# A gated state-space and convolution layer on one core: the last projection's two token parts become 336 and 240 columns wide, where they were 288 each

## The reference

```python
proj = x @ w_in                       # 2048 -> 10240, split into eight parts
y_a  = ssm_branch(u_a, ...)           # complex state space, GELU, GLU
y_a  = (y_a * silu(z_a)) @ w_out_a    # 1024 -> 2048
y_c  = conv_branch(b_c, c_c, h_c, ...)
y_c  = (y_c * silu(z_c)) @ w_out_c    # 1024 -> 2048
merged = sigmoid(g_a) * y_a + sigmoid(g_c) * y_c
out  = merged @ w_o                   # 2048 -> 2048, the last projection
r    = DN_ALPHA * x + out             # residual
mu   = mean(r); var = mean((r - mu)**2)        # over the 2048 features
y    = (r - mu) * rsqrt(var + 1e-5) * ln_g + ln_b
```

## Time and profile before

| | |
|---|---|
| median of three runs | 1619.18 us (1614.2 to 1620.25) |
| profiled execution | 1611.43 us, of which 1609.6 us are the span |
| TensorE busy | 1576.2 us, 98% of the span |
| VectorE busy | 820.9 us, 51% |
| ScalarE busy | 443.2 us, 28% |
| chain that ended last | TensorE 93%, VectorE 5% |
| first pass of the last projection | about 1378.0 to 1481.2 us |
| second pass | about 1481.2 to 1584.8 us |
| after the last matmul of a half | 1584.8 to 1609.6 us |

### The profile page before, as it was taken

One profiled execution on the slowest core, in us unless ns is written; L12 is line 12 of the kernel. 1 busy time (PEld: TensorE's weight loads), 2 busy tenths in 40 slices (PEclk: granted clock), 3 DMA queues, 4 the chain that ended last, 5 costly groups with the idle time before them and its releaser, 6 DMA issues.

```text
span 1609.6 us, 27311 instructions
## 1 busy us (share of the span) xinstructions
PE 1576.2 (98%) x11878; PEld 1571.0 (98%) x11878; DVE 820.9 (51%) x1148; ACT 443.2 (28%) x566; POOL 189.0 (12%) x348
## 2 busy tenths in 40 slices
PE   8999999999999999999999999999999999999994
PEld 8999999999999999999999999999999999999993
DVE  5976374464463563543533523123742355566887
ACT  4222222222222222222222222222421122333444
POOL 0110041131211311212212212010000000000000
PEclk9999999999999999999999999999999999999997
DMA  9352262352443543534634535244544433456572
GB/s 306 100 162 92 88 173 74 110 150 70 134 117 101 137 122 111 166 99 125 174 97 140 150 84 160 81 145 157 182 143 131 132 123 116 157 184 194 184 224 101
DMA packets 87448, 221.23 MB, mean 137 GB/s; under 512 B 19744, under 2 KB 28576, under 8 KB 87328
## 3 DMA queue, kind: packets, MB, share of 16 engines
q1 hardware_dynamic: 71456, 188.78, 37.1%
q0 software_dynamic: 15872, 30.70, 8.1%
HBM read 186.55 MB, written 28.16 MB: 133 GB/s over the span
## 4 chain that ended last, share of the span: by engine, by line
PE 93%; DVE 5%; SPq 1%; DMA 1%; issue 1%; ACT 0%; DVEq 0%
PE acc L618 88%; DVE w_lo L947 1%; SPq L404 1%; DMA w_raw<-in_w 1%; PE y_ps L662 0%; PE y_ps L663 0%; PE y_ps L661 0%; DVE r_all L1437 0%; PE y_ps L660 0%; PE y_ps L659 0%; PE v_ps L638 0%; PE v_ps L639 0%; PE v_ps L637 0%; PE y_ps L658 0%; DVE r_all L1436 0%
## 5 line engine op out<-in xcount | busy, mean ns | idle before, releaser
L618 PE MATMUL acc<-xh,w_hi 128*128 128x288 f32 x2560 | 556.0, 298 | 5.6 <-DVE xl L955 3.3
L618 PE MATMUL acc<-xl,w_hi 128*128 128x288 f32 x2560 | 553.4, 297 | 0.0
L618 PE MATMUL acc<-xh,w_lo 128*128 128x288 f32 x2560 | 552.5, 297 | 0.0
L947 DVE TENSOR_TENSOR w_lo<-w_raw,w_hi 128x1024 fp32r<-128x1024 f32 x263 | 321.6, 1224 | 408.1 <-ACT w_hi L736 406.5
L736 ACT ACTIVATE w_hi<-w_raw 128x1024 fp32r<-128x1024 f32 x263 | 277.8, 1058 | 607.3 <-PE acc L618 592.5
L618 PEld LDWEIGHTS acc<-xh,w_hi 128*128 128x128 f32 x2560 | 414.7, 190 | 8.1 <-issue 4.3
L618 PEld LDWEIGHTS acc<-xh,w_lo 128*128 128x128 f32 x2560 | 415.3, 190 | 0.0
L618 PEld LDWEIGHTS acc<-xl,w_hi 128*128 128x128 f32 x2560 | 415.2, 190 | 0.0
L618 PE MATMUL acc<-mh,w_hi 128*128 128x288 f32 x512 | 151.4, 296 | 0.0
L618 PE MATMUL acc<-mh,w_lo 128*128 128x288 f32 x512 | 150.7, 294 | 0.0
L618 PE MATMUL acc<-ml,w_hi 128*128 128x288 f32 x512 | 150.7, 294 | 0.0
(11 more groups left out here) (272 smaller groups left out, 1543.8 us busy)
## 6 DMA issues: line engine op xcount, KB each, us to landing
w_raw<-in_w SPq DMA_DIRECT2D x263, 512.0 KB, 3.8
sg_dram<-out_st SPq DMA_DIRECT2D x32, 288.0 KB, 4.5
v_sw<-v_st POOLq DMA_DIRECT2D x32, 144.0 KB, 4.9
gc_in<-sg_dram SPq DMA_DIRECT2D x16, 288.0 KB, 2.7
sz_in<-sg_dram SPq DMA_DIRECT2D x16, 288.0 KB, 2.8
x_in<-in_xT SPq DMA_DIRECT2D x32, 144.0 KB, 2.2
outT<-o_st SPq DMA_DIRECT2D x32, 144.0 KB, 1.8
mb<-mq_dram POOLq DMA_DIRECT2D x8, 512.0 KB, 6.9
```

The source lines that it names most:

```text
L618: ins = pe.matmul(acc[:, par, t, 0:TH], w, m[:, k0 + k, t * TH:(t + 1) * TH], start=first and k == 0 and n == 0, stop=last and k == KH - 1 ...
L947: dve.tensor_tensor(w_lo[h % NW][:, :], w_raw[:, h % NW, :], w_hi[h % NW][:, :].bitcast(F32), ALU.subtract).then_inc(lo_ready, 1)
```

## The change

The two token parts get the widths `TO = (336, 240)`. The part widths enter the matmuls of the last projection, the feature sums, and every VectorE and ScalarE operation on `r_all`, `pivot`, `sq`, `acc_d`, `acc_q`, `mean`, `rstd`, `mean_r` and `o_st`. The input slots `x_in` become four tiles of 336 columns, where they were two tiles of 576 used by halves. Each engine issues the same instructions in the same order as before; only their widths and the tiles' places differ. The halves of all earlier projections keep their two matmuls of 288 columns.

```diff
+TO = (336, 240)
-    x_in = [r(f"x_in{i}", [P, TOK]) for i in range(2)]
+    x_in = [r(f"x_in{i}", [P, TO[0]]) for i in range(4)]
-    o_st = r("o_st", [P, 8, TH])
+    o_st = r("o_st", [P, 8, TO[0]])
-    def of_half(x, t):
-        return x[:, t * TH:(t + 1) * TH]
+    def of_part_o(x, t):
+        return x[:, t * TO[0]:t * TO[0] + TO[t]]
     def x_slot(m):
-        return of_half(x_in[m % 4 // 2], m % 2)
+        return x_in[m % 4][:, 0:TO[m // KX]]
...
-        def half(h, par, mh_, ml_, k0, first, last, per_block=None, ts=(0, 1)):
+        def half(h, par, mh_, ml_, k0, first, last, per_block=None, part=None):
...
-                    for t in ts:
-                        ins = pe.matmul(acc[:, par, t, 0:TH], w, m[:, k0 + k, t * TH:(t + 1) * TH],
+                    for t in (0, 1) if part is None else (part,):
+                        at, n_ = (t * TH, TH) if part is None else (t * TO[0], TO[t])
+                        ins = pe.matmul(acc[:, par, t, 0:n_], w, m[:, k0 + k, at:at + n_],
...
-            dve.scalar_tensor_tensor(of_half(r_all[:, n, :], t), x_slot(m), ALPHA, acc[:, n % 2, t, 0:TH],
+            dve.scalar_tensor_tensor(of_part_o(r_all[:, n, :], t), x_slot(m), ALPHA, acc[:, n % 2, t, 0:TO[t]],
...
-            out = of_half(r_all[:, n, :], t)
-            link(dve.tensor_tensor(out, out, of_half(rstd, t), ALU.mult))
-            dve.tensor_tensor(out, out, of_half(mean_r, t), ALU.subtract).then_inc(norm_ready, 1)
+            out = of_part_o(r_all[:, n, :], t)
+            link(dve.tensor_tensor(out, out, of_part_o(rstd, t), ALU.mult))
+            dve.tensor_tensor(out, out, of_part_o(mean_r, t), ALU.subtract).then_inc(norm_ready, 1)
```

More of the change, by code:

```diff
@@ L483, in load_x @@
             t, n = divmod(m, KX)
-            sp.dma_start(x_slot(m), of_half(d["xT"][n], t)).then_inc(xin_loaded[m % 4], 16)
+            sp.dma_start(x_slot(m), of_part_o(d["xT"][n], t)).then_inc(xin_loaded[m % 4], 16)
         def store(m):
@@ L488, in store @@
             sp.wait_ge(out_ready, m + 1)
-            sp.dma_start(of_half(d["outT"][n], t), o_st[:, m % 8, :]).then_inc(y_out[m % 8], 16)
+            sp.dma_start(of_part_o(d["outT"][n], t), o_st[:, m % 8, 0:TO[t]]).then_inc(y_out[m % 8], 16)
         for m in range(4):
@@ L703, in sum_features @@
         def sum_features(ps, src, t):
-            return pe.matmul(ps[:, t, 0:TH], ones[:, :], of_half(src, t), start=True, stop=True)
+            return pe.matmul(ps[:, t, 0:TO[t]], ones[:, :], of_part_o(src, t), start=True, stop=True)
         def sums(t):
@@ L723, in _ @@
             half(h, h % 2, mh, ml, (u // 2) % 2 * KH, u % 4 < 2, u % 4 >= 2,
-                 merged_there if h in (H_O, H_O + 2) else None, ts=(t,))
+                 merged_there if h in (H_O, H_O + 2) else None, part=t)
         sums(1)
@@ L893, in square @@
             act.wait_ge(d_ready, t * KX + n + 1)
-            act.activation(of_half(sq[n % 2], t), of_half(r_all[:, n, :], t), ACT.Square).then_inc(sq_ready, 1)
+            act.activation(of_part_o(sq[n % 2], t), of_part_o(r_all[:, n, :], t), ACT.Square).then_inc(sq_ready, 1)
         def mean_of(t):
             act.wait_ge(sums_done, 2 * t + 1)
-            act.activation(of_half(mean, t), v_ps[:, t, 0:TH], ACT.Copy, scale=1.0 / D_MODEL).then_inc(mean_ready, 1)
+            act.activation(of_part_o(mean, t), v_ps[:, t, 0:TO[t]], ACT.Copy, scale=1.0 / D_MODEL).then_inc(mean_ready, 1)
         def root(t):
             act.wait_ge(var_ready, t + 1)
-            act.activation(of_half(rstd, t), of_half(rstd, t), ACT.Sqrt).then_inc(std_ready, 1)
+            act.activation(of_part_o(rstd, t), of_part_o(rstd, t), ACT.Sqrt).then_inc(std_ready, 1)
         def finish(t, n):
@@ L908, in finish @@
                 act.wait_ge(y_out[m % 8], 16 * (m // 8))
-            act.activation(o_st[:, m % 8, :], of_half(r_all[:, n, :], t), ACT.Identity, scale=ln_par[:, n, 0:1],
+            act.activation(o_st[:, m % 8, 0:TO[t]], of_part_o(r_all[:, n, :], t), ACT.Identity, scale=ln_par[:, n, 0:1],
                            bias=ln_par[:, n, 1:2]).then_inc(out_ready, 1)
@@ L918, in _ @@
                 act.wait_ge(pivot_sum, t + 1)
-                act.activation(of_half(pivot, t), v_ps[:, t, 0:TH], ACT.Copy, scale=1.0 / P).then_inc(pivot_ready, 1)
+                act.activation(of_part_o(pivot, t), v_ps[:, t, 0:TO[t]], ACT.Copy, scale=1.0 / P).then_inc(pivot_ready, 1)
                 square(t, 0)
@@ L1401, in take_d @@
         def take_d(t, n):
-            out, ad, aq, q = (of_half(x, t) for x in (r_all[:, n, :], acc_d, acc_q, sq[n % 2]))
-            dve.tensor_tensor(out, out, of_half(pivot, t), ALU.subtract).then_inc(d_ready, 1)
+            out, ad, aq, q = (of_part_o(x, t) for x in (r_all[:, n, :], acc_d, acc_q, sq[n % 2]))
+            dve.tensor_tensor(out, out, of_part_o(pivot, t), ALU.subtract).then_inc(d_ready, 1)
             dve.wait_ge(d_ready, t * KX + n + 1)
@@ L1419, in variance @@
         def variance(t):
-            r_, m_, mr = (of_half(x, t) for x in (rstd, mean, mean_r))
+            r_, m_, mr = (of_part_o(x, t) for x in (rstd, mean, mean_r))
             dve.wait_ge(sums_done, 2 * t + 2)
-            link(dve.tensor_scalar(r_, y_ps[:, t, 0:TH], 1.0 / D_MODEL, LN_EPS, ALU.mult, ALU.add))
+            link(dve.tensor_scalar(r_, y_ps[:, t, 0:TO[t]], 1.0 / D_MODEL, LN_EPS, ALU.mult, ALU.add))
             dve.wait_ge(mean_ready, t + 1)
```

## The result

Over 20 runs of each, the changed kernel has a median of 1624.78 us (1619.4 to 1628.19) beside 1614.33 us before; the ratio of the means is 1.0056, 95% interval 1.0043 to 1.0069 (one of the 20 executions before took 3953.66 us, counts as slow and is not in the ratio). The change makes the kernel slower by 7 to 11 us. The profiled execution has a span of 1617.6 us, 1609.6 before.

A forecast was written before the change was run, and what follows sets the result against it. TensorE was taken to bound both last-projection passes, with VectorE and ScalarE's loop taking over in the second; +15.4 + 0.2 - 3.0 - 1.9 + 0.2 - 0.2 - 2.7 = +8.0 us, giving 1627 us, range 1616 to 1633.

The forecast's parts named there:

- TensorE by width: Last projection's matmul pace on TensorE: 153.2 ns at 336 columns, 112 ns at 240.
- The floor: Least time between TensorE matmul starts, most likely set by each matmul's own weight load: 111.6 ns.
- First pass: Last projection's first pass: 768 wider matmuls add 15.4 us, block 0's wider pivot work adds 0.2 us.
- The loop takes over: Second pass, steps 6 to 28: VectorE and ScalarE need 71.6 us against TensorE's 61.9, so TensorE waits about 10 us.
- E(3) and E(31): Ends of TensorE's halves 3 and 31 in the second pass; forecast 85.5 us apart, where it was 88.5.
- The lead is gone at step 6: Second pass: TensorE's lead is used up when norm steps begin, so further loop slowness becomes TensorE waits.
- D(6) - E(3): Second pass, from the end of TensorE's half 3 to the start of VectorE's step 6: forecast 9.25 us.
- The end: After the second pass's last half: narrower VectorE, ScalarE, feature-sum and store work saves 2.7 us.
- TensorE stays the bound: Rival, second pass: TensorE remains the limit and the passes cancel, -2.2 us, 1617; chance 0.12.
- A column costs less: Rival, both passes: 0.093 ns per column instead of 0.417, so -1.9 us, 1617; chance 0.08.
- The waits cost the clock: Rival, second pass: TensorE's new waits of about 1 us lower its clock, +4 us, 1631; chance 0.12.
- 240 columns above the floor: Rival, second pass: 118 ns per matmul, a half of 2.84 us, 1628; within the forecast's joint chance of 0.68.

The follow-up runs named there:

- e4: Changed kernel with widths 224/352 instead of 336/240; last projection 241.0 us, ratio 1.0067 to the kernel before.
- e3: Changed kernel with the widths the other way round, 240/336; last projection 234.7 us, ratio 1.0015 to the kernel before.
- e9: Changed kernel without the first part's VectorE norms, ScalarE rounding before squaring, SyncE loading weights earlier; output partly unnormalised; 230.9 us in last projection, ratio 0.9995.
- e12: Kernel before (288/288) with ScalarE rounding before squaring and SyncE loading weights earlier; last projection 231.7 us, ratio 1.0000.
- e1: Changed kernel without the first part's normalising operations on VectorE, output partly unnormalised; last projection 237.2 us, ratio 1.0031 to the kernel before.
- e2: Changed kernel with ScalarE rounding the next tile before it squares; last projection 239.7 us, ratio 1.0045 to the kernel before.
- e5: e1 with SyncE's weight load issued ahead of its wait for the residual sum; last projection 233.6 us, ratio 1.0011 to the kernel before.
- e7: Changed kernel with ScalarE rounding first, earlier weight loads and the first part's norms on GpSimd; last projection 240.3 us, ratio 1.0058 to the kernel before.

## Why the prediction was right

- **TensorE by width**: 153.1 ns forecast as 153.2, 112.2 as 112. The floor, argued from matmuls of 72 columns, is shown by e4: 224 columns take as long as 240. That the weight load sets it stays argued; no run changed the load.
- **First pass +15.4 + 0.2**: +15.4. By the paces it is 768 x 19.8 ns = 15.2; the pivot's residual sum went from 0.47 to 0.52 us and its feature sum from 0.72 to 0.80.
- **The loop takes over**: steps of 4.07, 4.15, 2.10 and 1.75 us against 4.04, 4.15, 2.10 and 1.73; 71.1 us for 23 steps against 71.6. I had added 0.7 us for late loads, where the earlier trace rows have 0.5; nothing of it came, since the four kinds of steps alone add up to 71.2. e3 and e9 show that it is the loop: with the narrow part in the pass without norms, or with the loop loosened, TensorE runs through. The 10 us of waits forecast are the 9.8 us lost between E(3) and E(31), of which the view of waits names 6.1.
- **The lead is gone at step 6**: D(6) - E(3) = 1519.86 - 1510.68 = 9.18, forecast 9.25. E(3) to E(31) 85.1 against 85.5.
- **The end**: -3.0 against -2.7. The two pairs of feature sums took 0.75 + 1.12 us and now 0.67 + 0.57, so -0.6 instead of the -0.3 of the sum; the rest of the term was right. Both figures rest on the 1.12 us, which I had read as the pair's cost and which holds 0.5 us of low clock. At the full clock, by e12, the pairs give -0.1 and the whole end -2.5.
- **Sum**: +7.3 us in the last projection against +8.0, or +7.8 against e12. The span's own +8.0 meets the forecast to the digit by chance, since 0.7 of it arose ahead of the change and 0.5 is missing because the kernel before ended at the low clock. The ratio's interval, 6.9 to 11.1 us, holds all of these. The time of 1627 was the median of three runs plus 8; over 20 runs the kernel before has 1614.3, so the level was 5 us too high and the difference right.
- **Chances**: slower by over 0.5% had 0.45, same 0.52; the ratio is 1.0056, right at the bound, and its interval lies on both sides of 1.005.
- **Rivals**: *TensorE stays the bound* is out, nine waits. *A column costs less* is out: 336 columns cost 19.8 ns more than 288. *The waits cost the clock* is out: the granted clock was 1.00 in every stretch of the second pass. *240 columns above the floor* holds in small: 112 ns at the pass's start, 114 over 23 halves when nothing else holds TensorE (e9), not the 118 assumed, and hidden by the loop in the changed kernel.
- **What I did not see**: that a second loop, through SyncE's queue and the weight load, stood close behind the first. It didn't matter for the forecast, which needed the slowest loop alone, but e1 and e2 were expected wrongly for it. And the piece of 744 matmuls holds two halves of the second pass, which I had overlooked when I said that it would last 114 us; it lasts 112.1.

How full the loop was is not in the busy shares. The stretch of the 23 steps in the kernel before (us, busy us of PE, PEld, DVE, ACT, POOL; PEclk, DMA share, GB/s):

```profile
1505.20:1578.30 73.10, 73.10 (x558) 73.10 (x557) 62.35 (x104) 36.30 (x50) 0.00 (x0) 1.00 0.66 205
```

VectorE is busy for 62.35 of 73.1 us, 85%, and ScalarE for half; only the steps in order show that between them they leave 2%.

## What to carry to other kernels

When a stage's matmuls get shorter, the time of the other engines per tile becomes the limit, and it must be added up as a loop through their queues (here split, residual sum, square, rounding), not as busy shares: VectorE was 85% busy in those steps before, yet they filled 98% of TensorE's time. Two passes that trade work don't cancel when only one of them has slack: put the narrow part where the other engines have the least to do (worth 4.8 us here, e3, and still no gain over equal parts). Behind the loop that is removed stands the next; take them all away once, as in e9, to see what the idea is worth at most before working on them one by one.

## What was not expected of the hardware

- The fixed part of a matmul's pace beyond its columns at 2.4 GHz isn't constant: 13.3 ns (first part, 288 and 304 columns), 13.1 (336), 11.7 (second part, 288), 13.5 (272), 14.2 (240, e9), 13.3 (336 and 352 as second part). It repeats to 0.1 ns between kernels of the same widths (99.12 and 91.65 us for the two pieces of 288/288 both before and in e12); the cause is open, and none of the experiments was made for it.
- An idle stretch of 2.38 us ahead of the GLU was followed by a granted clock of 0.70 over 5 us before and by 1.00 in the changed kernel, from the same instructions. The last projection starts up to 12 us apart between profiled executions, more than the change moves. The clock goes with it: in the 33 executions of the kernel before that were run beside e9 to e12 the mean granted clock lies between 0.979 and 0.985, and 0.001 less goes with 1.2 us more (correlation -0.85). The earliest start, 1373.68 us, is e1's at a mean of 0.985, the latest, 1385.83 us, e5's at 0.980.
- VectorE's operations with two SBUF inputs take 1.4 times (the split of 1024 columns, the pivot's subtraction of 240) to 2.5 times (the running sums, 240) as long while GpSimd runs elementwise work (e7), and GpSimd itself needs 1.1 to 1.6 us for 336 columns, where VectorE needs 0.5.
